# The modulation weights are multiplied unsplit, in f32, in four column strips of the array

## The reference

```python
cond_x, cond_c = jax.nn.silu(c), jax.nn.silu(c_ctx)                 # 1024 numbers each
mx = jnp.split((cond_x @ mod_w[layer] + mod_b[layer])[:, None, :], N_MOD, axis=-1)   # mod_w: (2, 1024, 9216)
mc = jnp.split(cond_c @ mod_w[layer] + mod_b[layer], N_MOD, axis=-1)
...
x = x + 0.5 * mx[2] * swiglu(modulate(rms_norm(x, norm_g[layer, 0]), mx[0], mx[1]), ffn_w_in[layer, 0], ffn_w_out[layer, 0])
```

## Time and profile before

| | |
|---|---|
| median of three executions | 3116.46 us |
| span of the profiled execution | 3115.2 us |
| TensorE busy / weight loads busy | 2893.5 us / 2520.8 us |
| VectorE / ScalarE busy | 1721.5 us / 1232.1 us |
| HBM read | 389.49 MB, 125 GB/s over the span |

### The profile page before, as it was taken

One profiled execution on the slowest core, in us unless ns is written; L12 is line 12 of the kernel. 1 busy time (PEld: TensorE's weight loads), 2 busy tenths in 40 slices (PEclk: granted clock), 3 DMA queues, 4 the chain that ended last, 5 costly groups with the idle time before them and its releaser, 6 DMA issues.

```text
span 3115.2 us, 45778 instructions
## 1 busy us (share of the span) xinstructions
PE 2893.5 (93%) x17416; PEld 2520.8 (81%) x17416; DVE 1721.5 (55%) x2403; ACT 1232.1 (40%) x1488; POOL 0.2 (0%) x4
## 2 busy tenths in 40 slices
PE   7899899988998999699998898999989999889897
PEld 6888899987888999588886666888868888677897
DVE  6687667566866665624335645433353333566655
ACT  3364555443545554522323243323232232335443
POOL 0000000000000000000000000000000000000000
PEclk8999999999989999799999999999999999989998
DMA  7544467765444678224233201233232432320463
GB/s 222 157 151 153 154 210 232 220 174 149 156 143 155 211 231 232 75 70 123 74 95 87 81 1 54 75 98 111 76 86 82 115 94 79 103 68 23 135 189 101
DMA packets 584942, 393.06 MB, mean 126 GB/s; under 512 B 43670, under 2 KB 579124, under 8 KB 584628
## 3 DMA queue, kind: packets, MB, share of 16 engines
q1 hardware_dynamic: 584756, 390.57, 42.4%
HBM read 389.49 MB, written 1.05 MB: 125 GB/s over the span
## 4 chain that ended last, share of the span: by engine, by line
PE 83%; DVE 11%; ACT 4%; issue 2%; DMA 0%; SPq 0%; DVEq 0%; ACTq 0%
PE bank L1857 83%; DVE w_lo L1151 4%; ACT w_hi L837 2%; DVE t L1166 1%; DVE xs L1166 1%; DVE t L1159 1%; DVE rings L1166 1%; ACT t L841 0%; DVE acc L1159 0%; DVE h_lo L1166 0%; DMA raw<-in_w_in 0%; DVE score L1487 0%; DVE qk L1159 0%; DVE t L1163 0%; ACT gates L841 0%
## 5 line engine op out<-in xcount | busy, mean ns | idle before, releaser
L1151 DVE TENSOR_TENSOR w_lo<-raw,w_hi 128x2048 fp32r<-128x2048 f32 (+3 forms) x410 | 853.9, 2083 | 397.1 <-ACT w_hi L837 395.2
L837 ACT CAST w_hi<-raw 128x2048 fp32r<-128x2048 f32 (+3 forms) x410 | 711.8, 1737 | 691.6 <-PE bank L1857 673.2
L1857 PE MATMUL bank<-h_hi,w_hi 128*128 128x512 f32 (+1 forms) x1560 | 573.2, 367 | 51.0 <-DVE h_lo L1166 41.0
L1857 PE MATMUL bank<-h_hi,w_lo 128*128 128x512 f32 (+1 forms) x1560 | 569.1, 365 | 0.0
L1857 PE MATMUL bank<-h_lo,w_hi 128*128 128x512 f32 (+1 forms) x1560 | 568.1, 364 | 0.0
L1857 PE MATMUL bank<-x_hi,w_hi 128*128 128x256 f32 x1344 | 385.1, 287 | 20.1 <-DVE x_lo L1166 13.0
L1857 PEld LDWEIGHTS bank<-h_hi,w_hi 128*128 128x128 f32 x1560 | 297.3, 191 | 105.4 <-issue 47.8
L1857 PE MATMUL bank<-x_hi,w_lo 128*128 128x256 f32 x1344 | 378.9, 282 | 0.0
L1857 PE MATMUL bank<-x_lo,w_hi 128*128 128x256 f32 x1344 | 378.6, 282 | 0.0
L1857 PEld LDWEIGHTS bank<-h_hi,w_lo 128*128 128x128 f32 x1560 | 296.6, 190 | 49.8
L1857 PEld LDWEIGHTS bank<-h_lo,w_hi 128*128 128x128 f32 x1560 | 297.3, 191 | 47.8
(11 more groups left out here) (282 smaller groups left out, 4332.0 us busy)
## 6 DMA issues: line engine op xcount, KB each, us to landing
raw<-in_ffn_w_in SPq DMA_DIRECT2D x176, 512.0 KB
raw<-in_mod_w SPq DMA_DIRECT2D x72, 1024.0 KB
raw<-in_ffn_w_out SPq DMA_DIRECT2D x64, 704.0 KB
raw<-in_w_in SPq DMA_DIRECT2D x40, 1024.0 KB
raw<-in_w_ff_in SPq DMA_DIRECT2D x32, 1024.0 KB
raw<-in_w_ff_out SPq DMA_DIRECT2D x32, 1024.0 KB
raw<-in_w_out SPq DMA_DIRECT2D x8, 1024.0 KB
raw<-in_w_ple_gate SPq DMA_DIRECT2D x8, 1024.0 KB
```

The source lines that it names most:

```text
L837: act.copy(w_hi[s][:, w], raw[s][:, w]).then_inc(hi_made, c.did(hi_made))
L1151: dve.tensor_tensor(w_lo[s][:, w], raw[s][:, w], w_hi[s][:, w].bitcast(F32), ALU.subtract).then_inc(lo_made, c.did(lo_made))
L1857: ins = pe.transpose(o, l, r) if transpose else pe.matmul(o, l, r, start=start, stop=stop)
```

## The change

The modulation chunk is no longer split. ScalarE and VectorE prepare main chunks only, in w slots of their own count (main chunk m in slot m modulo 3; `position(m)` gives the raw slot). TensorE waits for the landing of the modulation chunk and multiplies straight from `raw`, in plain f32: eight matmuls, one for each k tile, each with a stationary operand of 32 columns, of which two are the vectors; k tile k goes to the strip k modulo 4 of the array's columns, and so to partitions 32·(k mod 4) and up of the bank, where tiles k and k+4 are summed. The turn then sums the four strips by a `fold` with ones at rows 0, 32, 64, 96 and 1, 33, 65, 97, over 128 rows. The calls of `advance(m)` on ScalarE are gone. The raw slot of a modulation chunk is free once TensorE has used it (`mod_used`); for the main chunks it is `lo_made` as before.

```diff
+STREAM1 = stream1()
+MAIN_POS = [p for p, (kind, _) in enumerate(STREAM1) if kind != "mod"]
+MOD_POS = [p for p, (kind, _) in enumerate(STREAM1) if kind == "mod"]
+def position(m):
+    return MAIN_POS[m] if m < MAINS1 else CHUNKS1 + m - MAINS1 if m < LAYERS * MAINS1 else m + LAYERS * MODS
-    out["fold"] = np.tile(np.eye(2, dtype=f), (P // 2, 1))
+    out["fold"] = (np.arange(P)[:, None] % (P // COL_GROUPS) == np.arange(2)[None, :]).astype(f)
-        cond_st = fixed("cond_st", [P, 4 * KT + P - 4], F32R)
+        cond_st = fixed("cond_st", [P, KT, P // COL_GROUPS])
...
+            def slot_free():
+                before = n[0] - SLOTS
+                if before >= LAYERS * CHUNKS1:
+                    sp.wait_ge(lo_made, c.value(lo_made, before - LAYERS * MODS + 1 + SLOTS))
+                    return
+                turn = before // CHUNKS1
+                kind, what = STREAM1[before % CHUNKS1]
+                if kind == "mod":
+                    sp.wait_ge(mod_used, c.value(mod_used, MODS * turn + what + 1 + 1))
+                else:
+                    m = MAIN_POS.index(before % CHUNKS1)
+                    sp.wait_ge(lo_made, c.value(lo_made, MAINS1 * turn + m + 1 + SLOTS))
             def chunk(pieces):
                 s = n[0] % SLOTS
-                sp.wait_ge(lo_made, c.value(lo_made, n[0] + 1))
+                slot_free()
...
-                    s = n[0] % SLOTS
-                    act.wait_ge(landed[s], c.value(landed[s], LANDED * (n[0] // SLOTS + 1)))
+                    at, s = position(n[0]), n[0] % SLOTS
+                    act.wait_ge(landed[at % SLOTS], c.value(landed[at % SLOTS], LANDED * (at // SLOTS + 1)))
                     act.wait_ge(chunk_used, c.value(chunk_used, n[0] + 1))
                     w = slice(0, WIDTHS[n[0]])
-                    act.copy(w_hi[s][:, w], raw[s][:, w]).then_inc(hi_made, c.did(hi_made))
+                    act.copy(w_hi[s][:, w], raw[at % SLOTS][:, w]).then_inc(hi_made, c.did(hi_made))
...
-                    passed()
                     j = m // 2
                     dve.wait_ge(d_full, c.next(d_full))
...
-                    copy(mod_rows[0:4, :], b[0:4, 0:256]).then_inc(d_free, c.did(d_free))
+                    copy(mod_rows[:, :], b[:, 0:256]).then_inc(d_free, c.did(d_free))
...
-                    w = parts(chunk(), KT, 256)
+                    at = MOD_POS[m // 2]
+                    pe.wait_ge(landed[at % SLOTS], c.value(landed[at % SLOTS], LANDED * (at // SLOTS + 1)))
+                    w = raw[at % SLOTS][:, :].rearrange("p (k n) -> p k n", k=KT)
...
                     for k in range(KT):
-                        for z in range(2):
-                            mm(b[:, 0:256], cond_st[:, 4 * k:4 * k + P], w[z][:, k, :], k == 0 and z == 0, k == KT - 1 and z == 1,
-                               d_full if k == KT - 1 and z == 1 else None)
+                        strip = slice(P // COL_GROUPS * (k % COL_GROUPS), P // COL_GROUPS * (k % COL_GROUPS + 1))
+                        mm(b[strip, 0:256], cond_st[:, k, :], w[:, k, :], k < COL_GROUPS, k >= KT - COL_GROUPS,
+                           d_full if k == KT - 1 else None)
-                    owed[0] = True
+                    owed[0] = mod_used
```

More of the change, by code:

```diff
@@ L100 @@
 MODS = 36
-CHUNKS1 = len(MAIN) + MODS
-assert len(MAIN) == 2 * MODS and CHUNKS1 % SLOTS == 0
+MAINS1 = len(MAIN)
+CHUNKS1 = MAINS1 + MODS
+assert MAINS1 == 2 * MODS and CHUNKS1 % SLOTS == 0 and MAINS1 % SLOTS == 0
+COL_GROUPS = 4
 def stream1():
@@ L196, in chunk_widths @@
     ffn += [HT * P] * KT
-    stages = [([size[kind] for kind, _ in stream1()], LAYERS), (ffn, 2), ([2048] * 3 + [KT * P] + [2048] * 9, 1),
+    stages = [([size[kind] for kind, _ in MAIN], LAYERS), (ffn, 2), ([2048] * 3 + [KT * P] + [2048] * 9, 1),
               (ffn, 2), (ffn, 2), ([2048] * 11, 1), (ffn, 2)]
@@ L644, in build @@
         x_tile, tile_squared, acc_ready = sem("x_tile"), sem("tile_squared"), sem("acc_ready")
-        cond_exp, cond_ready, cond_hi_made, cond_lo_made = (
-            sem(n) for n in ("cond_exp", "cond_ready", "cond_hi_made", "cond_lo_made"))
+        cond_exp, cond_ready, cond_made = (sem(n) for n in ("cond_exp", "cond_ready", "cond_made"))
+        mod_used = sem("mod_used")
         p_room, p_copied, p_hi_made, p_lo_made = (sem(n) for n in ("p_room", "p_copied", "p_hi_made", "p_lo_made"))
@@ L727, in up @@
                         (view(slot, 3, 512)[0:HALF, 2, :], src[256:320, cols])]
-                for k, (kind, what) in enumerate(stream1()):
+                for k, (kind, what) in enumerate(STREAM1):
                     if k == 6:
@@ L894, in _ @@
             do(ACT.Exp, t3[:, 0, 0:16].rearrange("p (c k) -> p c k", c=2), cond[:, :, :], scale=-1.0).then_inc(cond_exp, c.did(cond_exp))
-            act.wait_ge(cond_ready, c.next(cond_ready))
-            act.wait_ge(c.last, c.own())
-            do(ACT.Copy, cond_cols[:, 0:2, :], cond[:, :, :]).then_inc(cond_hi_made, c.did(cond_hi_made))
             def sigmoid(o):
@@ L1147, in prep @@
                 while n[0] <= upto:
-                    s = n[0] % SLOTS
+                    s, r = n[0] % SLOTS, position(n[0]) % SLOTS
                     dve.wait_ge(hi_made, c.value(hi_made, n[0] + 1))
                     w = slice(0, WIDTHS[n[0]])
-                    dve.tensor_tensor(w_lo[s][:, w], raw[s][:, w], w_hi[s][:, w].bitcast(F32), ALU.subtract).then_inc(lo_made, c.did(lo_made))
+                    dve.tensor_tensor(w_lo[s][:, w], raw[r][:, w], w_hi[s][:, w].bitcast(F32), ALU.subtract).then_inc(lo_made, c.did(lo_made))
                     n[0] += 1
@@ L1207, in _ @@
             dve.wait_ge(c.last, c.own())
-            copy(cond_st[:, 4 * KT:], raw[0][:, 0:P - 4]).then_inc(v_step, c.did(v_step))
+            dve.memset(cond_st[:, :, :], 0.0).then_inc(v_step, c.did(v_step))
             dve.wait_ge(c.last, c.own())
@@ L1925, in _ @@
             pe.wait_ge(phase_in, 16)
-            pe.wait_ge(cond_hi_made, c.next(cond_hi_made))
-            pe.wait_ge(cond_lo_made, c.next(cond_lo_made))
+            pe.wait_ge(cond_made, c.next(cond_made))
             def layer_norm_sums():
```

81 lines of the change are left out of this document (39 added, 42 removed).

## The result

The changed kernel takes 3365.28 us (median of four executions, 3360.68 to 3374.24) where the kernel before takes 3116.31 us: ratio 1.0804, 95% interval 1.0783 to 1.0825. That is slower, as forecast, but by 249 us where 124 were forecast, and outside the range of 3180 to 3325 us.

What follows compares the result with a forecast made beforehand. The prediction took TensorE as the bound, 83% of the chain. Late-load losses less TensorE's savings summed to 62 us per layer, 124 for both, on a median of 3116.46: forecast 3240 us, range 3180 to 3325.

Steps and rivals of the forecast that it cites:

- Rival B: Modulation matmuls: the strips run one behind the other, a chunk costs 4.5 instead of 1.9 us; 3375 us in all, chance 0.11.
- Rival C: TensorE's clock: new waits leave it idle, so it falls to half speed, through whole rounds; 3310 us in all, chance 0.10.
- Saving where TensorE is the bound: Rounds bounded by TensorE: the unsplit modulation chunk takes 1.94 instead of 2.72 us, a round 13.14 instead of 13.92.
- Landing of the queued chunks: The two main chunks queued behind SP's modulation load land at T + 8.1 and T + 11.2; second product T + 8.7 and T + 12.2.
- T: The moment TensorE's first matmul after a modulation chunk ends; only then may SP issue the next modulation chunk.
- the bound that the prediction gave and did not use: Landing of a third chunk between 11.2 and 12.7 us after T: 1.5 us on 12 rounds a layer, up to +36.
- Query and key: Query and key tiles and output, 5 rounds: VectorE's copy frees the bank late, +2.7 us each, 13.5 per layer.
- Second product: MLP's second product: residual sum behind both w_lo, at T + 16.5; +3.4 us for seven rounds, 23.8 per layer.
- Single places M10, M30, M34, M39: VectorE stands in front of a first main chunk until T + 12.4: +6.3, +5.4, +6.9 and +4.4, together 23.0 us per layer.
- Attention: Attention rounds: ScalarE's casts delay ReLUs in the first two, +2 and +7; the seven others 0; together +9 us per layer.
- First product: MLP's first product, 8 rounds: ScalarE empties the banks, so TensorE stays the bound; -0.78 us each.
- End of the layer: Eighth round of the MLP's second product, ending in the layer norm, where VectorE came late before too: +0.6 us.

Runs made afterwards that it cites:

- order: The changed kernel with SP's order altered alone: each modulation chunk's load is issued behind two main chunks instead of ahead of them; 3043.69 us.
- serial: On top of order, all eight f32 matmuls of a modulation chunk go to the first strip of 32 columns, turn over 32 rows; 3228.1 us.
- dcount: The changed kernel with the kernel before's places of preparation on VectorE alone; ScalarE still casts two main chunks ahead at once; 3250.1 us.
- count: The changed kernel with the places of preparation of the kernel before on both ScalarE and VectorE; 3135.3 us.
- shift: The kernel before with 384 unused bytes behind cond_st, moving everything behind it in SBUF, no other edit; 3127.8 us.
- both: As place, but with the first network's activations alone put 384 bytes further on; 3035.6 us.
- best: The kernel both with the places of preparation of count; 3077.0 us.
- late: The kernel before, products still split, but SP's load into the third slot waits until TensorE has left the modulation chunk, not for its w_lo; 3244.7 us.
- place: The kernel order with cond_st as narrow as before the change, so that what lies behind it keeps its old SBUF addresses; 3038.6 us.

## Why the prediction was wrong

**What held.** The direction, and the mechanism in query and key tiles and the MLP's second product: SP's wait, the two main chunks behind it, the landing, VectorE ahead of the bank. The products of a chunk: 0.86 us were forecast for four records one behind the other, and the 16 records start in groups of four, 0.22 us apart, the last 0.69 us behind the first. By the Trainium skill ("TensorE: Matmul & The Clock Gate", Part 3), 2.38x for three strips, it would have been an estimated 1.1 us; here 3.57 us became 1.00 with four strips, 3.6x, in f32 at 256 columns. Rival B falls with this.

**Rival C is not gone.** In the second product the clock does fall (0.83 in its stretch), but the loads set the round: TensorE has been idle for 3.78 us when it begins. Elsewhere it may have cost. The first network from its first modulation chunk on, before, changed and order:

```profile
43.80:1253.80 1210.00, 1142.10 (x8696) 1076.26 (x8695) 830.06 (x1119) 585.06 (x618) 0.00 (x0) 0.96 0.61 183
43.20:1477.70 1434.50, 1135.30 (x8694) 1023.21 (x8694) 670.26 (x1044) 449.93 (x545) 0.00 (x0) 0.86 0.51 154
42.70:1148.50 1105.80, 1033.96 (x8691) 937.26 (x8694) 668.68 (x1043) 445.66 (x545) 0.00 (x0) 0.96 0.66 199
```

Of the 329 us between changed and order, 227 are idle TensorE, and for 101 it is busy longer with the same matmuls, at a granted clock of 0.86 in place of 0.96. How much of these 101 the late loads would have taken anyway, had the clock stayed up, no run separates.

**Saving where TensorE is the bound: forecast 0.78 us a round, measured 1.48.** Order's rounds are 12.44 against 13.92. From the main matmul ahead of the turn to the one behind the chunk it is 2.72 before and 0.11 + 0.43 + 1.00 = 1.54 now: the switches beside the turn shrank too, which I had kept (0.18 ahead of the first product, 0.33 behind the last). The one ahead of the turn and of the product comes back when serial's turn takes 32 rows again. The other 0.3 is the pace.

**Landing of the queued chunks: forecast T + 8.7 and T + 12.2 in the second product, measured T + 9.6 and T + 13.7.** The spacing of the earlier trace rows was of two chunks; a third behind them, in rows of 512 bytes, came later. (The measured ones are means of 12 rounds.) Part of it is one straggler: 14 of the 16 parts of the second main chunk landed by 684.94, the 15th at 685.58, the last at 686.32. In that end, the second row here, the 16 DMA engines are busy for 0.07 of the time, about one of them on the mean:

```profile
674.00:684.50 10.50, 10.50 (x82) 10.50 (x82) 0.21 (x1) 1.90 (x1) 0.00 (x0) 0.89 1.10 297
684.50:686.50 2.00, 2.00 (x28) 1.56 (x26) 2.00 (x1) 0.09 (x1) 0.00 (x0) 1.00 0.07 20
```

A packet of 16 KB of the instruction queue lies at 680.94 and takes 1.19 us of one engine. Over the first network the last part came 0.71 us behind the 15th in the 72 loads with an instruction packet in their time, and 0.12 us in the 139 without; the two go together, but no run took the packets away. Of the query and key chunks, issued in one or two pieces more, the third landed at T + 11.8 to 12.0 or T + 13.3 to 14.0, not 11.2. That makes 1.5 us on the mean over 12 rounds of a layer, the bound that the prediction gave and did not use.

**Single terms, us per layer (layer 0).** Query and key, M3 to M9: forecast 4 x 2.7 = 10.8, measured 20.4. Second product, seven rounds: 23.8 and 37.7. Single places M10, M30, M34, M39: 23.0 and 28.0. Attention: 9 and 28.0. First product: -6.2 for eight rounds and +1.4. End of the layer: 0.6 and 4.2. (The ends of the first matmuls of M30 and M38 had been taken 0.11 us too late, 0.39 for rows that say 0.28; nothing hangs on it.) With the small rest, layer 0 is 113 us longer up to its last modulation chunk, and its end with layer 1 another 112; the forecast was 62 for each layer.

**The step that failed most: attention at +9, and in it ScalarE's queue.** ScalarE's cast waits for the same late landing, in order, ahead of the ReLUs that empty a bank. In attention of layer 0 TensorE's waits for these ReLUs (`rings`) add up to 2.7 us before, 13.5 in the changed kernel, 14.8 in dcount, where VectorE's places are put back and ScalarE's are not, and 2.5 in count. The rest of the 28 us are longer waits for VectorE (`gates` 9.3 us where it was 2.8, `o_lo` 8.6 where it was 2.2) and a slower clock (0.86, before 0.98: TensorE is busy 170.4 us there, and 153.6 with the same instructions in order, where it was 0.99). I had followed VectorE's queue behind the new wait at every place and ScalarE's only in two steps of attention.

**The first product: forecast -6.2, measured +1.4.** "Here ScalarE empties the banks, so TensorE stays the bound" held for the banks: TensorE waits for none of them there. What failed is "The first main chunk is ready by then; that wait alone costs nothing". It landed at T + 8.3 to 10.0 (forecast 8.1), cast and subtraction put its `w_lo` at T + 12.6 to 14.3, and TensorE, faster than forecast, was back near T + 12. So it waits for `w_lo`, in layer 0 seven times and 8.7 us in all, for instance:

```profile
498.49 0.38 PE L1873 MATMUL bank<-x_hi,w_hi 128*128 128x256 f32 x1 [1.86 <-DVE w_lo L1169]
```

**The second network: forecast 0, measured +33.** Its instructions are the same, but 20.6 us come from 384 bytes of address (shift), and about 5.5 from the late chunks at its start (the layer norm's first matmul 8.6 instead of 3.1 us behind the last product with modulation weights). Some 7 us stay open; the mean granted clock is 0.95 there where it was 0.96.

**The parts together.** The first network in us, by when the loads come and where the main chunks are prepared, with unsplit products throughout:

| | two chunks ahead at once | places of before |
|---|---|---|
| loads late | 1477.7 (changed) | 1238.8 (count) |
| loads ahead | 1148.5 (order), 1154.9 (both) | 1209.7 (best) |

Late loads cost 329 us with the new places and 29 with the old ones. Preparing two main chunks ahead costs 239 while the loads are late, and gains 55 once they are ahead (both against best). Neither half of the change makes the loss alone. With split products late loads alone cost 115.6 us (late). Late and count differ by 131: TensorE is busy 1172.4 us in the one and 1065.5 in the other, 107 less, which is what 72 savings of 1.48 come to, and idle some 22 us less. The old places on ScalarE alone were not tried: by the written order ScalarE and VectorE would then wait for each other.

## What to carry to other kernels

A slot that is released later holds more than its own load: look at what stands behind that wait in the queue, and move the loads that don't need it ahead. How far ahead an in-order engine prepares is worth choosing only together with how early the data comes: the same choice cost 239 us here and gained 55. When an edit changes the size of a buffer, keep the addresses of the others, or time the shift by itself.

## What the runs showed that I had not expected

- The pace of back-to-back f32r matmuls depends on where the activations lie in SBUF: 226.8 to 233.3 ns for 512 columns and 114.5 to 119.4 for 256, over offsets of 0 to 384 bytes. What in the addresses does it wasn't found. It is not one pace per address: in place the rounds of the MLP are 12.42 or 12.85 us and nothing between, in both nearly all 12.44. Nor are the activations all of it, since the kernel before, with the same offset as place, has a mean of 117.4 ns where place has 116.2.
- A chunk has landed only when the last of its 16 parts has, and in the loads with an instruction packet of 8 or 16 KB in their time that last part comes 0.71 us behind the 15th, otherwise 0.12 us. That the packet holds it up is likely (the one of 16 KB took an engine 1.19 us) but not shown.
- In the hardware loop, SP's first load of the next pass was issued 5.5 us behind the last one of a pass (561.52 to 567.06 in order); where the last waits for TensorE, that gap shows at the layer's end.
